# Forty dense first keys instead of thirty-two in a two-block kernel's expert layers

## The reference, cut to what matters

```python
s1 = q[:, 0] @ keys1.T                 # 128 first keys
s2 = q[:, 1] @ keys2.T                 # 128 second keys
v1, i1 = top_k(s1, 16); v2, i2 = top_k(s2, 16)
top, pos = top_k(v1[:, None] + v2[None, :], 16)     # 16 of 256 pairs
e = i1[pos // 16] * 128 + i2[pos % 16]              # one of 16384 experts
g = softmax(top)
y += sum_k g[k] * gelu(down[e[k]] . x) * up[e[k]]   # rows of 2048 numbers
```

## Time and profile before

| | |
|---|---|
| median of 3 runs | 3850.77 us (3848.56 to 3855.85) |
| the profiled execution | span 3851.0 us |
| steps 16 to 275 of the first expert layer | 1125 to 2252 us of the span |
| the same of the second | 2754 to 3845 us |
| busy: PE, DVE, POOL, ACT | 85%, 67%, 32%, 20% of the span |
| granted TensorE clock, mean | 0.918 |

### The profile page before, as it was taken

How to read it: one execution, slowest core, us unless ns; L and a number is a source line. 1 busy time by engine, 2 the same in 40 slices (tenths; PEclk the granted TensorE clock), 3 DMA queues, 4 the chain that set the end, 5 groups by cost and what they waited for, 6 DMA issues and landing times.

```text
span 3851.0 us, 41880 instructions
## 1 busy us (share of the span) xinstructions
PE 3268.2 (85%) x14020; PEld 1670.6 (43%) x14020; DVE 2594.4 (67%) x5278; ACT 751.7 (20%) x1759; POOL 1249.4 (32%) x1133
## 2 busy tenths in 40 slices
PE   8998998899998887556888899999988875578888
PEld 7343344444785554111222258557855531122222
DVE  3877785565668889997555431525788889975563
ACT  1222223410111114642000001221110146510000
POOL 0000000000125455566454400002254555665553
PEclk9999999999999998667899999999999986689999
DMA  6343433235579999899999974424899998999998
GB/s 223 114 117 108 120 117 100 98 109 197 198 297 398 397 398 392 336 361 382 363 391 396 375 245 131 149 103 188 306 402 391 384 360 307 373 371 389 378 387 322
DMA packets 316855, 1075.61 MB, mean 279 GB/s; under 512 B 94332, under 2 KB 103436, under 8 KB 214668
## 3 DMA queue, kind: packets, MB, share of 16 engines
q0 software_dynamic: 147456, 728.77, 48.7%
q1 hardware_dynamic: 134240, 335.05, 24.5%
q10 hardware_dynamic: 34960, 9.27, 1.1%
HBM read 1415.93 MB, written 2.10 MB: 368 GB/s over the span
## 4 chain that ended last, share of the span: by engine, by line
PE 47%; DMA 23%; DVE 19%; issue 7%; SPq 2%; POOL 2%; ACT 1%; ACTq 0%; DVEq 0%; POOLq 0%; another core or an unknown queue 0%
PE bank L746 9%; DMA big<-in_peer_down,sc 7%; PE bank L1170 7%; DMA big<-in_peer_u,sc 7%; DMA wring<-in_dense_up 6%; DVE sc L2389 5%; PE bank L760 4%; PE bank L1109 4%; DVE sc L2392 4%; PE bank L1231 4%; PE bank L987 3%; PE bank L1153 2%; PE bank L911 2%; PE bank L976 2%; POOL big L680 2%
## 5 line engine op out<-in xcount | busy, mean ns | idle before, releaser
L2389 DVE CUSTOM_DVE_ANT_0 sc<-big,hs 128x1024 f32<-128x1024 f32 x480 | 588.0, 1225 | 433.1 <-DMA big<-in_peer_down,sc 218.0
L1231 PE MATMUL bank<-big,sc 128*32 128x512 f32 x4096 | 633.6, 703 | 175.9 <-DMA big<-in_peer_up,sc 85.2
L1170 PE MATMUL bank<-wring 128*128 128x512 f32 x1024 | 534.6, 658 | 122.8 <-DMA wring<-in_dense_up 100.7
L2392 DVE CUSTOM_DVE_ANT_0 sc<-big,hs,sc 128x1024 f32<-128x1024 f32 x480 | 616.9, 1285 | 17.2
L1153 PE MATMUL bank<-ht,wring 128*128 128x256 f32 x2048 | 504.3, 398 | 0.9 <-ACT wring L1639 0.9
L1153 PEld LDWEIGHTS bank<-ht,wring 128*128 128x128 f32 x2048 | 389.0, 196 | 191.2 <-issue 138.6
L746 PE MATMUL bank<-wring,ht 128*128 128x512 f32 x1024 | 471.5, 615 | 0.0
L680 POOL DMA_INDIRECT big<-in_peer_down,sc x256 | 305.1, 1192 | 365.3 <-DVE sc L2392 226.7
L680 POOL DMA_INDIRECT big<-in_peer_u,sc x256 | 309.6, 1210 | 304.8 <-DVE sc L2392 154.1
L680 POOL DMA_INDIRECT big<-in_peer_v,sc x256 | 306.0, 1195 | 277.8 <-PE bank L1231 169.5
L1170 PEld LDWEIGHTS bank<-wring 128*128 128x128 f32 x1024 | 189.8, 201 | 461.3 <-issue 330.9
(11 more groups left out here) (432 smaller groups left out, 3507.2 us busy)
## 6 DMA issues: line engine op xcount, KB each, us to landing
wring<-in_w_in SPq DMA_DIRECT2D x84, 1024.0 KB, 5.7
wring<-in_dense_down SPq DMA_DIRECT2D x64, 1024.0 KB
wring<-in_dense_up SPq DMA_DIRECT2D x256, 256.0 KB
wring<-in_w_out SPq DMA_DIRECT2D x32, 1024.0 KB, 5.2
wring<-in_w_attn_o SPq DMA_DIRECT2D x16, 1024.0 KB, 5.0
wring<-in_peer_w_query SPq DMA_DIRECT2D x16, 1024.0 KB, 8.9
wring<-in_peer_w_q SPq DMA_DIRECT2D x16, 1024.0 KB, 6.9
wring<-in_glu_w_a SPq DMA_DIRECT2D x8, 1024.0 KB, 5.1
```

The source lines that it names most:

```text
L1170: mm = pe.matmul(dense_out[t][:, :], dense_w[:, r, t * P:(t + 1) * P], sup[:, m % 2, r % 4, :], start=(r == 0), stop=(r == DENSE - 1))
L1231: mm = pe.matmul(acc_bank[j][32 * q:32 * q + 32, :], w_blocks[:, u % 2, g, :], gslot[:, m % RING, q * 512:(q + 1) * 512], start=(u % PH == ...
L2389: st.link(v.tensor_tensor_reduce(dot_out[:, 0:cut_at], row[:, 0:cut_at], h[:, u // PH, 0:cut_at], 1.0, start, ALU.mult, ALU.add, acc))
L2392: v.tensor_tensor_reduce(dot_out[:, cut_at:D], row[:, cut_at:D], h[:, u // PH, cut_at:D], 1.0, start, ALU.mult, ALU.add, acc).then_inc(dot ...
```

## The change

`DENSE` goes from 32 to 40 in both layers. The first product runs 2 parts a step instead of 1.5 and so ends at step 94, the second 5 parts in 3 steps instead of 4, and ends at step 267 as before. The gates are multiplied the other way round: the 128 second keys are the stationary operand and the 40 first-key rows the moving one, so that the product comes out with the second key on the partitions, as `dense_w` has it. The copy by ACT and the transpose by PE go away with their semaphores, and DVE takes each batch of 8 tokens straight from its bank (32 times 320 numbers instead of 16 times 512). `dense_w` needs 2048 more columns; `wring` gets them, and the memory comes from the area that holds the descriptors of POOL's DMAs, which is halved.

```diff
-DENSE = 32
+DENSE = 40
 def quarter_at(n):
-    return min(4 + max(n - TOPK, 0) * 3 // 2, 4 * DENSE)
+    return min(4 + max(n - TOPK, 0) * 2, 4 * DENSE)
 def up_part_at(n):
-    return min(max(n - FIRST_UP, 0) * 4 // 3, 4 * DENSE)
+    return min(max(n - FIRST_UP, 0) * 5 // 3, 4 * DENSE)
...
-        wring = sb("wring", SLOTS * SLOT)
+        wring = sb("wring", SLOTS * SLOT + 2048)
...
             def dense_gates(layer, hb):
...
-                if hb % 2 == 0 and n >= 4:
-                    pe.wait_ge(gate_copied, n // 2 - 1)
+                if n >= 2:
+                    pe.wait_ge(gate_evac, n - 1)
                 for j in range(GATE_T):
-                    q, col = j % 4, (hb % 2 * 2 + j // 4) * P
-                    mm = pe.matmul(bank[32 * q:32 * q + 32, col:col + P], hot_a[:, hb % 2, j, :], hot_b[:, hb % 2, j, :],
-                                   start=True,
-                                   stop=True, skip_group_check=True)
+                    mm = pe.matmul(dense_out[hb % 2][:, j * DENSE:(j + 1) * DENSE], hot_b[:, hb % 2, j, :],
+                                   hot_a[:, hb % 2, j, :], start=True, stop=True, skip_group_check=True)
                 mm.then_inc(hot_mm, 1)
-            def turn_gates(layer, b):
...
-            def copy_gates(layer, b):
...
-            def take_gates(layer, b):
+            def take_gates(layer, hb):
-                v.wait_ge(gate_done, layer * GRP + b + 1)
+                v.wait_ge(hot_mm, layer * NT * GATE_N + hb + 1)
...
-                v.tensor_tensor(w, gate_bank[:, 0:16 * DENSE].rearrange("p (n r) -> p r n", r=DENSE), w,
+                v.tensor_tensor(w, dense_out[hb % 2][:, 0:GATE_T * DENSE].rearrange("p (n r) -> p r n", r=DENSE), w,
                                 ALU.mult).then_inc(gate_evac, 1)
...
-                    hb = gate_batch_at(n - 3)
-                    if hb is not None and hb % (16 // GATE_T) == 16 // GATE_T - 1:
-                        take_gates(layer, hb // (16 // GATE_T))
+                    if gate_batch_at(n - 2) is not None:
+                        take_gates(layer, gate_batch_at(n - 2))
...
-    nc = _bacc.Bacc("TRN2", target_bir_lowering=False, num_devices=1)
+    nc = _bacc.Bacc("TRN2", target_bir_lowering=False, num_devices=1,
+                    dynamic_dma_scratch_size=8192)
```

More of the change, by code:

```diff
@@ L189, in two_blocks @@
         cn = sb("cn", 976)
-        wslot = wring[:, :].rearrange("p (s c) -> p s c", s=SLOTS)
+        wslot = wring[:, 0:SLOTS * SLOT].rearrange("p (s c) -> p s c", s=SLOTS)
         gslot = big[:, :].rearrange("p (s c) -> p s c", s=SLOTS)
@@ L319, in two_blocks @@
         hot_mm = sem("dense_gates_multiplied")
-        gate_copied = sem("dense_gates_copied")
-        gate_done = sem("dense_gates_done")
         gate_evac = sem("dense_gates_evacuated")
@@ L414, in two_blocks @@
         key_n = big[:, 12288:14336].rearrange("p (h s c) -> p h s c", h=PH, s=2)
-        kscore = wring[:, 8192:12288]
+        kscore = wring[:, 10240:14336]
         dense_w = wring[:, 0:DENSE * T].rearrange("p (r n) -> p r n", r=DENSE)
[L417 to L421, removed]
+        sdn = wring[:, 14336:18432].rearrange("p (b c) -> p b c", b=2)
+        sup = wring[:, 14336:18432].rearrange("p (b r c) -> p b r c", b=2, r=4)
+        hot_b = wring[:, 10240:10240 + 2 * GATE_T * P].rearrange("p (i n c) -> p i n c", i=2, n=GATE_T)
+        hot_a = wring[:, 12288:12288 + 2 * GATE_T * DENSE].rearrange("p (i n c) -> p i n c", i=2, n=GATE_T)
         (rW2, rCA, rCB, rV, rIF, rTP, rPF, rIU, rPU, rP2, rIX, rIM, rGT, rSS, rAC, rGE, rWT, rWR, rDI2, rUI, rGM, rTM,
@@ L430, in two_blocks @@
         selT = sub(rSL).rearrange("p (t a n) -> p t a n", t=NT, a=3)
-        keyT = [w.rearrange("p (j c) -> p j c", j=PH) for w in (wring[:, 14336:15360], sub(rBL))]
+        keyT = [w.rearrange("p (j c) -> p j c", j=PH) for w in (wring[:, 16384:17408], sub(rBL))]
         pqT = sub(rSL).rearrange("p (k n) -> p k n", k=3)
@@ L438, in two_blocks @@
         first_scores = kscore.rearrange("p (t h s c) -> p t h s c", t=NT, h=PH, s=2)[:, :, :, 0, :]
-        squares = wring[:, 12288:14336].rearrange("p (t h c) -> p t h c", t=NT, h=PH)
+        squares = wring[:, 14336:16384].rearrange("p (t h c) -> p t h c", t=NT, h=PH)
         acc_bank, dense_out, turn_bank, gate_bank = psum[0:4], psum[4:6], psum[6], psum[7]
@@ L1163, in up_part @@
                     pe.wait_ge(dd_evac, (layer + 1) * (DENSE // 2))
-                    pe.wait_ge(gate_evac, (layer + 1) * GRP)
+                    pe.wait_ge(gate_evac, (layer + 1) * NT * GATE_N)
                 if r == 0 and c:
@@ L1188, in turn_selections @@
                 if t:
-                    pe.wait_ge(gate_evac, layer * GRP + GRP // 2)
+                    pe.wait_ge(sel_ready, 2 * (layer * NT + 1))
                 for j in range(3):
@@ L1194, in dense_gates @@
             def dense_gates(layer, hb):
-                n, bank = layer * NT * GATE_N + hb, dense_out[hb // 2 % 2]
+                n = layer * NT * GATE_N + hb
                 pe.wait_ge(first_hot, n + 1)
@@ L1243, in expert_products @@
                     u, g = divmod(n - FIRST_DOWN, GRP)
-                    if gate_batch_at(n - 2) is not None and gate_batch_at(n - 2) % 2:
-                        turn_gates(layer, gate_batch_at(n - 2) // 2)
                     if gate_batch_at(n) is not None:
@@ L1690, in peer_units @@
                             dense_gelu(layer, p)
-                        if gate_batch_at(n) is not None and gate_batch_at(n) % 2:
-                            copy_gates(layer, gate_batch_at(n) // 2)
                         if gate_batch_at(n + 3) is not None:
@@ L2349, in decode_gates @@
                 mine = slice(u * TOPK, (u + 1) * TOPK)
-                match = sc[:, rW2[0]:rCA[1]].rearrange("p (k r) -> p k r", k=TOPK)
+                match = sc[:, rW2[0]:rW2[0] + TOPK * DENSE].rearrange("p (k r) -> p k r", k=TOPK)
                 st.link(v.tensor_tensor(match, tok_sel[:, t, 0, cols].unsqueeze(2).broadcast_to([P, TOPK, DENSE]),
@@ L2455, in first_one_hots @@
                                 ALU.is_equal).then_inc(first_hot, 1)
-            def take_gates(layer, b):
-                v.wait_ge(gate_done, layer * GRP + b + 1)
-                if b == 0:
+            def take_gates(layer, hb):
+                v.wait_ge(hot_mm, layer * NT * GATE_N + hb + 1)
+                if hb == 0:
                     v.wait_ge(dd_evac, (layer + 1) * (DENSE // 2))
-                w = dense_w[:, :, b * 16:(b + 1) * 16]
-                v.tensor_tensor(w, gate_bank[:, 0:16 * DENSE].rearrange("p (n r) -> p r n", r=DENSE), w,
+                w = dense_w[:, :, hb * GATE_T:(hb + 1) * GATE_T]
+                v.tensor_tensor(w, dense_out[hb % 2][:, 0:GATE_T * DENSE].rearrange("p (n r) -> p r n", r=DENSE), w,
                                 ALU.mult).then_inc(gate_evac, 1)
```

## The result

The changed kernel takes 3990.87 us (median of 4 runs, 3979.53 to 3995.20) against 3853.31 for the kernel before beside it: a ratio of 1.0343, 95% interval 1.0324 to 1.0362. It is 3.4% slower. The forecast was 1.1% slower, 3893 us, with a range up to 3945: the direction was right, and the size was not.

The account below looks back on a forecast made before the run. DMA was taken as the main limit with PE close behind, and DVE as pacing the gates. First product +33, gates -4, second product 0 and tail +13 gave +42 us on 3851.0: 3893 us, range 3825 to 3945.

Parts of the forecast that it names:

- The first product: First product of both layers: PE becomes the limit at 4.70 us a step, +33 us for both.
- The 0.08 us a step for waits: First product: waits above the floor as PE, DMA and DVE meet in one chain of 8 slots, 6 us.
- The five steps behind the last part: First product, steps 94 to 98 without a dense part: go at DVE's pace, 4.04 us each, 20.2 us.
- Rival 1: Whole kernel: DMA stays the limit and PE keeps up, so it gets faster, 3830 down to 3814 us; chance 0.20.
- The gates: Gate stretch: DVE's extra work +6 a layer, less the later DMA saving; -4 us for both layers, bounds +16 and -20.
- The saving of 9 and 7 us in the last 24 steps: End of the gate stretch, set by DMA: fewer rows save 0.36 us a step, -9 and -7 us by layer.
- rival 4: Gates: PE is the limit at the low clock, by 0.3 us over 64 steps, +19 a layer, 3931 us; chance 0.08.
- The second product: Second product: DMA's saving of 9 and 10 us offset by 10 for late loads; 0 for both, bounds -19 and +130.
- rival 3: Second product: dense `up` rows come late, the double buffer takes over, some 30 us a layer more, 3953 us; chance 0.12.
- The tail: Steps 256 to 267, PE without gaps: 11 steps get a third of a part more, +13 us for both layers.
- The bytes: DMA over the whole kernel: 8744 fewer rows save 181 us, sixteen more keys cost 90, so 91 us less.
- The halved area: Descriptor area of POOL's DMAs: halving costs nothing, since eight gathers in flight are all it ever holds.

Follow-up runs that it names:

- the new gates alone: Changed kernel put back to 32 keys and the old pace, keeping the new gate order and halved descriptor area: 3861.14 us, ratio 1.0014.
- one-part slots: Dense `up` rows in eight slots of one part, not two buffers of four: changed kernel (40 keys) 3863.08 us; kernel before (32 keys) 3839.11 us.
- the pace alone: Changed kernel with 32 keys but the new pace (2 parts a step, 5 in 3): 3966.30 us, ratio 1.0274.
- the earlier issue: Changed kernel where SP reads the four key numbers before waiting for the buffer, so its four DMAs go out closer together: 3956.42 us, ratio 1.0264.
- the dummies: Changed kernel with four dummy matmuls of 512 columns ahead of 16 waits for dense `up` rows a layer: 3970.44 us, ratio 1.0291.

## Why the prediction missed

**The first product: right in kind, too high in size.** The forecast made PE the limit at 4.70 us a step, with DMA just below it at 4.60 and 4.54. The trace has 4.66 to 4.69 in most stretches of eight steps, PE 99.6% busy, the clock at 1.00. The stretch from first to last matmul was forecast as 370 us:

```profile
L1150 PE MATMUL bank<-ht,wring x1280: 379/379/483, 1127.4 to 1497.3; 128*128 128x256 f32 x183
...
L1150 PE MATMUL bank<-ht,wring x1280: 379/379/483, 2828.6 to 3197.2; 128*128 128x256 f32 x183
```

It took 369.9 and 368.6, against the earlier trace rows before. The 0.08 us a step for waits, 12 us of the 33, did not come about. The five steps behind the last part, forecast at 20.2 us, took 19.3 and 15.8. So it is +12.6 us to step 96, or +11.5 to step 99, where the forecast's own stretch ends, and not +33. Rival 1 falls here: two parts cost 4.65 as the earlier trace rows had them. Another 12 us come a few steps later, up to step 106. The Trainium skill's way to judge PE's room by the busy share of weight loads (Perfetto Trace Analysis, Identifying the Most-Contended Engine) shows 204.04 / 302 = 68% in this window, where PE has no gap and sets the pace. The measurement decides: here the distance between starts was the better measure.

**The gates: near the forecast by another cut.** DVE's new durations are as forecast (medians from the trace):

```profile
L2436 DVE TENSOR_TENSOR wring<-bank,wring x64: 480/487/493, 1529.4 to 3502.9; 128x320 f32<-128x320 f32 x64
L2426 DVE TENSOR_TENSOR wring<-sc x64: 471/482/493, 1513.4 to 3490.2; 128x320 f32<-128x320 f32 x64
```

By the starts of DVE's own dot products, steps 96 to 152, which DVE sets, grew by 6.1 and 7.1 us, as forecast (+6), and over the whole span its busy time grew by 19.7 us (2594.4 to 2614.1), 9.9 a layer where 7.8 were forecast. The saving of 9 and 7 us in the last 24 steps came to 8.1 and 3.5 by PE's starts, and to less than 1 by DVE's. Of the +23.7 up to step 106 most goes with the pace: with 32 keys it brings 17.0 over the new gates alone. Why the steps just behind the quicker first product are slow was not taken apart.

PE's new matmuls, priced at 1.8 to 4.5 us a batch, take 1.98 even here, where the granted clock of the window is 0.63, and rival 4 falls:

```profile
1602.24 1.98 PE L1203 MATMUL bank<-wring 128*128 128x40 f32 x16 [1.50 <-DVE wring L2426]
```

**The second product: the step that failed.** The prediction put its late loads as "I take 10, since the loads get a larger share of the engines when the ring is full", between 0 and 74 us a layer, and set that off against DMA's saving for a sum of 0. Measured: +91, 47.9 and 43.1 us. Two things were wrong.

The first is the lateness. The trace before had what a load takes: SP issues one at 1957.56, and PE, which waits for it, starts at 1972.16, 14.6 us later:

```profile
1957.56 3.68 SPq L574 DMA_DIRECT2D wring<-in_dense_up  x4
1972.16 2.93 PE L1170 MATMUL bank<-wring 128*128 128x512 f32 x4 [3.91 <-DMA wring<-in_dense_up]
```

Over the loads that PE waited for there, the median is 15.6 us in layer 1 and 15.0 in layer 2, and none took less than 13.3. The prediction knew the total of the waits, but never set this time beside the 11.1 us that it gave a load. The loads did get quicker, as it expected: in the changed kernel the medians are 13.4 and 12.6. But the time at hand fell by more, from 14.2 to 11.1. The bound was low as well, since 80 steps at the new pace hold 33 loads and not 24: 3.1 us for each are 103 a layer.

The second is the overlap, and it decides. PE's need of 4.05 us a step was compared with DMA's 4.63 without the waits. At the old pace 80 steps need 278 us of PE; with 50.8 us of waits that is 329, well inside the 380 that DMA took, and so the waits cost nothing. At the new pace they need 324. With 66.6 us of waits, and 1.7 us more for each of 15 parts that ran at the lower clock, which was not in the sum at all, that is 416 by this rough sum: more than the 370 that DMA would have taken, and near the 427.5 measured in layer 1. PE's idle time in this stretch didn't grow (70.5 us before, 67.0 after); it stopped being free.

The mechanism had been named (rival 3, chance 0.12), and its condition, loads that land more than 11 us after their buffer is free, was met by the trace before already. Its price, 30 us a layer, was too low as well. The runs show the cause: the one-part slots take away the waits and 118 us of the second product's time with the same memory and the same bytes, more than the whole 91; the pace alone, without more keys, brings 105; the earlier issue gives 34 and the dummies 20.

**The tail** was forecast at +13 and is +22.1. With the one-part slots it is +13.5, so the rest goes with the late loads.

**The bytes** were counted right, the time for them was not: 657.17 MB in POOL's queue where 131072 - 50884 rows of 8192 bytes are 656.9, and 368.61 in SP's:

```profile
q0 software_dynamic: 147456, 657.17, 44.3%
q1 hardware_dynamic: 145760, 368.61, 26.3%
```

Share times span is the DMA engines' time: 1875 + 943 us before and 1767 + 1049 in the changed kernel, the same sum within 3 us, where 91 us less were forecast. The first term was too high, 181 us for the gathers and 108 measured (128 with one-part slots), and SP's too low, 90 us and 106 measured (96). The rows that are still fetched take longer: a packet of 8192 bytes in POOL's queue has a mean of 331 ns before, 345 in the changed kernel and 341 with one-part slots. Why is open. So even with good slots DMA's time falls by some 30 us and not by 91, and it can be saved only where DMA is the limit. With good slots, 40 keys against 32 gain 4.7 and 9.2 us in the second product, and lose 3.8 and 3.1 in the first, where PE is the limit, 8.7 and 7.0 in the gates, where DVE is, and 8.4 and 6.8 in the tail, where PE is again: 24 us in all. **The halved area** was rightly costed at nothing.

**The sum.** The direction was right partly by luck. Without the second product the terms add up to +47 where +42 were forecast, with the first product 20 us too high and the gates and the tail 26 too low.

## What to carry to other kernels

When a change quickens the pace at which a buffer is used, compare two times before anything else: how long a refill takes from the free buffer to its first use, issues included, and how long the other buffers last at the new pace. Where the refill is longer, add the waits to what the engine needs for its own work, and only then compare with the engine that sets the pace. The waits in the old trace are no measure of their cost: in a stretch that DMA sets they can lie inside DMA's own time, as the kernel with 32 keys and one-part slots showed (6 to 7 us a layer for 50 us of waits), and they begin to cost when the waiting engine's own work grows. Where the two times are close, refill in the smallest piece that is used: eight slots of one part did in the same memory what two buffers of four could not, and won 128 us at the new pace.

## What was not expected of the hardware

- SP needs 1.1 us for each DMA whose address it first reads from memory, when that read stands between the DMAs; with the four reads ahead of the wait, the four DMAs go out in 1.6 us from first to last instead of 3.3.
- In the first layer's second product of the changed kernel PE waited 2.5 to 6.0 us for dense rows 15 times, and each time the next part, two matmuls of 512 columns, took 3.45 to 3.78 us instead of 1.98, as at 1.2 GHz and not 2.4. With PE kept busy through the waits the window's mean clock was 0.98 instead of 0.90, and the program 20 us faster in spite of the added matmuls.
- With fewer gathered rows and more rows of dense keys, a gathered row's packet of 8192 bytes took 345 ns in the mean instead of 331, so that 10% fewer rows saved 6% of their time.
- Halving the descriptor area of POOL's DMAs did not change the time (0.9999), with a ring of eight gathers of 128 rows.
